# Attention steps inside a feed-forward loop: the weighted sum before the maximum, and finished outputs handled as an item begins

## The reference

```python
def _diff_attend(q1, q2, k1, k2, v, q_pos, k_pos, lam):
    ...
    def probs(q, k):
        s = jnp.einsum('bqhd,bkhd->bhqk', q.astype(jnp.float32), k.astype(jnp.float32)) * scale
        return jax.nn.softmax(jnp.where(mask, s, NEG_INF), axis=-1)

    w = probs(q1, k1) - lam * probs(q2, k2)
    return jnp.einsum('bhqk,bkhe->bqhe', w, v.astype(jnp.float32))
...
    f = (jax.nn.silu(h @ lw['ffn_w_gate']) * (h @ lw['ffn_w_up'])) @ lw['ffn_w_down']
```

## Time and profile before

| | us |
|---|---|
| median of 3 runs | 3170.92 |
| lowest, highest | 3169.41, 3175.09 |
| profiled execution, its own time | 3174.06 |
| its span | 3172.3 |
| PE busy | 2966.4 (94%) |
| DVE busy | 1779.2 (56%) |
| ACT busy | 1375.5 (43%) |
| POOL busy | 220.2 (7%) |

### The profile page before, as it was taken

One profiled execution on the slowest core, in us unless ns is written; L12 is line 12 of the kernel. 1 busy time (PEld: TensorE's weight loads), 2 busy tenths in 40 slices (PEclk: granted clock), 3 DMA queues, 4 the chain that ended last, 5 costly groups with the idle time before them and its releaser, 6 DMA issues.

```text
span 3172.3 us, 38465 instructions
## 1 busy us (share of the span) xinstructions
PE 2966.4 (94%) x14384; PEld 2413.3 (76%) x14384; DVE 1779.2 (56%) x2858; ACT 1375.5 (43%) x2500; POOL 220.2 (7%) x314
## 2 busy tenths in 40 slices
PE   6999999759999999999999999899999999999997
PEld 5788787547768777777877787778788777787875
DVE  5767745357626666566565556655666555333454
ACT  4655635344224444554444445544444444222233
POOL 0101100110000000001000100001111000000000
PEclk9999989868999999999999999999999999999998
DMA  5546332546754443454443334534332244232221
GB/s 159 182 140 222 133 134 73 150 135 228 217 150 116 123 113 113 154 159 120 116 114 105 108 101 155 162 103 130 100 114 76 96 167 126 80 97 84 86 74 59
DMA packets 377720, 402.65 MB, mean 127 GB/s; under 512 B 25657, under 2 KB 277989, under 8 KB 377536
## 3 DMA queue, kind: packets, MB, share of 16 engines
q1 hardware_dynamic: 360768, 341.38, 36.5%
q0 software_dynamic: 16768, 58.81, 4.8%
HBM read 341.26 MB, written 58.91 MB: 126 GB/s over the span
## 4 chain that ended last, share of the span: by engine, by line
PE 60%; DVE 11%; ACT 3%; issue 2%; DMA 0%; SPq 0%; DVEq 0%; ACTq 0%; POOL 0%; POOLq 0%
PE c_bank L2582 48%; PE b_S L2874 3%; PE b_WT L2886 2%; DVE c_w L2262 2%; PE b_O L2900 2%; DVE b_m L2462 1%; PE b_S L2591 1%; PE b_O L2591 1%; ACT c_junk L2034 1%; DVE c_rows L2273 1%; DVE c_rows L2280 1%; PE b_S L2854 1%; PE b_O L2902 1%; DVE c_act L2374 1%; DVE b_p L2469 1%
## 5 line engine op out<-in xcount | busy, mean ns | idle before, releaser
L2582 PE MATMUL c_bank<-c_hT,c_w 128*128 128x512 f32 (+1 forms) x4416 | 1036.8, 389 | 14.9 <-DVE c_hT L2300 14.9
L2582 PEld LDWEIGHTS c_bank<-c_hT,c_w 128*128 128x128 f32 x4416 | 802.0, 192 | 171.9 <-issue 17.7
L2262 DVE TENSOR_TENSOR c_w<-c_raw,c_w 128x1024 fp32r<-128x1024 f32 x334 | 405.5, 1220 | 198.2 <-ACT c_w L2013 196.9
L2582 PE MATMUL c_bank<-c_w,c_fT 128*128 128x512 f32 x2112 | 506.7, 393 | 0.0
L2013 ACT ACTIVATE c_w<-c_raw 128x1024 fp32r<-128x1024 f32 x334 | 351.1, 1055 | 290.2 <-PE c_bank L2582 246.3
L2582 PEld LDWEIGHTS c_bank<-c_w,c_fT 128*128 128x128 f32 x2112 | 391.7, 188 | 87.3 <-issue 3.4
L2191 ACT ACTIVATE b_p<-b_S,b_nm 128x512 f32<-128x512 f32 (+3 forms) x288 | 180.0, 630 | 518.6 <-DVE b_nm L2463 518.6
L808 PE MATMUL a_bank<-a_w,a_hT 128*128 128x512 f32 (+1 forms) x1224 | 300.1, 401 | 0.0
L2582 PE MATMUL c_bank<-c_w,c_hT 128*128 128x512 f32 x1152 | 270.4, 393 | 7.7 <-DVE c_w L2262 4.0
L808 PEld LDWEIGHTS a_bank<-a_w,a_hT 128*128 128x128 f32 (+1 forms) x1224 | 220.6, 183 | 61.3 <-issue 3.8
L2582 PEld LDWEIGHTS c_bank<-c_w,c_hT 128*128 128x128 f32 x1152 | 217.9, 190 | 54.8 <-DVE c_w L2262 4.4
(11 more groups left out here) (362 smaller groups left out, 3391.2 us busy)
## 6 DMA issues: line engine op xcount, KB each, us to landing
c_raw<-in_ffn_w_gate SPq DMA_DIRECT2D x88, 512.0 KB, 4.9
c_raw<-in_ffn_w_up SPq DMA_DIRECT2D x88, 512.0 KB, 4.1
c_raw<-in_ffn_w_down SPq DMA_DIRECT2D x88, 512.0 KB, 4.3
a_raw<-in_w_in SPq DMA_DIRECT2D x40, 1024.0 KB, 5.1
b_k<-split_kT SPq DMA_DIRECT2D x72, 256.0 KB, 4.9
b_v<-split_v SPq DMA_DIRECT2D x36, 512.0 KB, 3.6
c_raw<-in_w_out SPq DMA_DIRECT2D x32, 512.0 KB, 5.0
c_raw<-in_ple_w_gate SPq DMA_DIRECT2D x32, 512.0 KB, 4.4
```

What stands on the lines that cost most here:

```text
L2262: V.tensor_tensor(w[:, e[1] % SLOTS, 1], raw[:, n % RAW], w[:, e[1] % SLOTS, 0].bitcast(F32), ALU.subtract).then_inc(split_ready, 1)
L2582: ins = T.matmul(out, lhs(k, a), rhs(k, b), start=first and k == 0 and n == 0, stop=end and k == blocks - 1 and n == 2)
```

## The change

In both attention stages VectorE's weighted sum of the older step moves ahead of the maximum of the new one. In `feed`, the copy `ob` and the addition to `o` of a finished tile move from behind the transposed weights to the very top of the item, on ScalarE and on VectorE; the square and the root stay behind the transposed weights but go ahead of the copy `fT` of the feed-forward block. No instruction is added or taken away.

```diff
@@ attend_first, vector @@
             for t in range(END):
+                s = t - ADD
+                if 0 <= s < NSTEP:
+                    i, kc, n = tile_of[s], STEPS[s][3], size(s)
+                    dve.wait_ge(t2_ready, s + 1)
+                    V.scalar_tensor_tensor(p[:, s % PRING, 0, 0:n], p[:, s % PRING, 0, 0:n], coef[:, i % TRING, 0, kc:kc + 1],
+                                           p[:, s % PRING, 1, 0:n], ALU.mult, ALU.add).then_inc(w_ready, 1)
                 if t < NSTEP:
...
-                s = t - ADD
-                if 0 <= s < NSTEP:
...
@@ feed, scalar @@
+                x = finished(n, 1)
+                if x is not None:
+                    act.wait_ge(pv_done, last_step[x] + 1)
+                    wait_if_any(act, o_ready, x)
+                    A.activation(ob[:], O[:, 0, 1], ACT.Copy).then_inc(ob_ready, 1)
                 if was == ("mix0", 3):
...
                     A.activation(wT[:, 0, 0:size(s)], WT[:, 0:size(s)], ACT.Copy).then_inc(wt_hi, 1)
-                if was[0] in ("up", "far"):
-                    b = was[1]
-                    bank, count = job[j, "up", b]
-                    act.wait_ge(acc_free[bank], count)
-                    A.activation(fT[:, b % 8, 0], act1[:, b % 2], ACT.Copy).then_inc(f_hi, 1)
                 x = finished(n, 1)
                 if x is not None:
-                    act.wait_ge(pv_done, last_step[x] + 1)
-                    wait_if_any(act, o_ready, x)
-                    A.activation(ob[:], O[:, 0, 1], ACT.Copy).then_inc(ob_ready, 1)
                     act.wait_ge(o_ready, x + 1)
...
+                if was[0] in ("up", "far"):
+                    b = was[1]
+                    bank, count = job[j, "up", b]
+                    act.wait_ge(acc_free[bank], count)
+                    A.activation(fT[:, b % 8, 0], act1[:, b % 2], ACT.Copy).then_inc(f_hi, 1)
@@ feed, vector @@
+                x = finished(n, 1)
+                if x is not None:
+                    dve.wait_ge(ob_ready, x + 1)
+                    if x >= 4:
+                        dve.wait_ge(o_turned, x // 4)
+                    V.tensor_tensor(o[:, x % 4], O[:, 0, 0], ob[:], ALU.add).then_inc(o_ready, 1)
                 if was == ("mix0", 3) and last:
...
+                s = valued(n)
+                if s is not None:
+                    g, h, t, kc = STEPS[s]
+                    x, c = tile_no(g, h, t), size(s)
+                    dve.wait_ge(t2_ready, s + 1)
+                    V.scalar_tensor_tensor(p[:, s % PRING, 0, 0:c], p[:, s % PRING, 0, 0:c], coef[:, x % TRING, 0, kc:kc + 1],
+                                           p[:, s % PRING, 1, 0:c], ALU.mult, ALU.add).then_inc(wc_ready, 1)
                 s = scored(n)
                 if s is not None:
...
                     V.tensor_scalar(nm[:, x % TRING, :, kc], m[:, x % TRING, :, kc], -QSCALE, None, ALU.mult).then_inc(nm_ready, 1)
-                s = valued(n)
-                if s is not None:
...
                 x = finished(n, 1)
-                if x is not None:
-                    dve.wait_ge(ob_ready, x + 1)
-                    if x >= 4:
-                        dve.wait_ge(o_turned, x // 4)
-                    V.tensor_tensor(o[:, x % 4], O[:, 0, 0], ob[:], ALU.add).then_inc(o_ready, 1)
                 s = scored(n)
```

## The result

The changed kernel took 3207.81 us (median of 4 runs, 3205.02 to 3209.07) beside 3170.44 for the kernel before (4 runs, 3169.41 to 3175.09): ratio 1.0114, 95% interval 1.0096 to 1.0131. It is slower by 37 us; the forecast was 20 slower, 3191, with 3173 to 3209 as its range, so the time lies 1 us inside the upper end. The profiled execution's span went from 3172.3 to 3205.9 us, by 33.6.

The account below looks back on a forecast made before the run. Largest single cause of TensorE's waits: transposes waiting for VectorE's weighted sum, 41.0 us in 35 waits. Terms: 19 + 16 + 3 - 13 - 5 = +20 us, giving 3191 us against the median, range 3173 to 3209.

Parts of the forecast that it names:

- the step: ScalarE's queue: `ob` at the top delays tanh and weight copy; value products wait 30 to 50 us for the low half.
- Finishing items after "up": 20 items right after a query tile's last value products, with tanh: tanh starts late, 0.96 us each, 19 us lost.
- The other finishing items: 24 items without tanh: weight copy behind `ob`, value products 0.72 us late each; 16 us lost (8 to 19).
- Heads: Four items after "up" that finish a head's fourth tile: `fT` behind the root costs 0.8 us each, 3 us lost.
- Rival 3: Slower by more: new stops halve the clock after them in each of 20 items, 31 us more, 3222 us; chance 0.05.
- The five long waits and the clock: TensorE's transposes where head outputs were just turned: 2.5 us gained from shorter waits, 5 us from less slow clock.
- The swap elsewhere: Sum ahead of maximum, outside finishing items: 4.8 us gained in eight other waits, 3.4 in a dozen late steps.
- First stage: `attend_first`, 16 steps with the sum ahead of the maximum: no net effect, 0 us, 4.8 either way.
- Rival 1: Faster: sum ahead of maximum pays in full, early finish is covered; 35 us gained, 3136 us; chance 0.12.
- Rival 2: No change: the 24 finishing items without tanh cost nothing, their weight copy being otherwise covered; +4 us, 3175 us; chance 0.12.
- rival 4: Moving the sum gains nothing, since it waits for POOL where it waited for the maximum; 3209 us; chance 0.03.

Follow-up runs that it names:

- the two kernels with the finish in the middle: Changed kernel with `ob` behind tanh and split, addition behind maximum, `fT` ahead of square and root: 3144.34 us; the same with maximum ahead of sum: 3162.62 us.
- the swap alone: Kernel before with only the weighted sum moved ahead of the maximum, in both attention stages: 3175.58 us, ratio 1.0012.

## Why the prediction was right, and where its sizes were off

The direction, the mechanism and the signs named beforehand came true: the wait for the sum fell to 26.2 (forecast 20 to 28), a wait for the low half appeared, 28.5 us (just under the forecast's 30 to 50, well over the 15 that would have spoken against the step), tanh stands behind `ob` and the products behind the addition. One part of a sign did not: behind tanh the wait for the sum was to grow, and in the items after "up" it went from 9.7 us to 9.2; the loss there shows at the value products, 12.4 us where there was none, and at the heads' turnings. The forecast came out 17 us low: 11 of it lie in the terms below, some 2 outside the items; the rest is what the profiled executions stand off their medians. That the time still lies in the range, by 1 us, is partly luck: two terms went past their own upper bounds (the other finishing items 20.7 against 19, the heads 8.1 against 5), while the items after "up" came out near their lower one. The range's lower end was also added up wrongly: it takes 19 for the items after "up", whose own lower bound is 15, and by its own terms would be -1, or 3170.

- *Finishing items after "up", 19.* Right in its chain, a little high: from tanh to the value products 8.00 us (forecast 8.10), from scores 8.37 (8.59), mostly because tanh starts 0.17 after the copy does and not after its end. 0.74 each instead of 0.96.
- *The other finishing items, 16.* Measured 20.7. The chain was right, but the durations came from items in which POOL was not busy. The 18 plain ones lose 17.1 us; with POOL's product cut they lose 12.4, 0.69 each against the forecast's 0.72. The moved instructions now fall beside POOL's.
- *Heads, 3.* This is the term that failed most. I took 0.8 in each of four items for `fT` behind the root; undoing that place alone brought 8 us, 5.6 of them in these heads and their turnings. The stop at the turning grew (1.62 to 2.09 us in the head shown, beside the new 0.60 ahead of it), and the clock fell where it had not fallen before: 17 us at the lower level in the ten items of this row of the table, none before the change. Rival 3 had this mechanism in the wrong place: not in all 20 items but at the turnings, where the stops are longest. That the pair of stops lowers the clock is read from these rows, not tried by itself.
- *The five long waits and the clock, 2.5 + 5.* Measured 7.4. The waits fell from 3.7 to 2.35 us; time at the low level in these items fell from 17 to 10 us, not to nothing, and the waits gave the rest.
- *The swap elsewhere, 8.* Measured 5.5; the three short turnings' 2 were lost under the late heads. The swap's full size is shown where nothing stands in its way, 18 us between the two kernels with the finish in the middle.
- *First stage, 0.* Shown.

Rival 1 (faster) was to be decided on VectorE, to whose chain the finish was to add no more than 0.53 us. By the item shown and that of the earlier trace rows it adds 1.53: the first product with tanh starts 1.08 us after the scores (1033.11 and 1032.03), where it started 0.45 ahead of them. The run with both steps in the middle adds nothing ahead of the sum, and is faster, by 29 us where the rival had 35. Rival 2 fell with the other finishing items, rival 4 with the wait's fall; in the change the sum waits 0.0 us for POOL.

I was wrong about the swap alone, after the prediction, and the reading comes from the prediction itself: it calls the 1.20 us at the low half the only cover of the chain. In a finishing item the addition comes later still and releases the same value products; there the cover was 0.40 us. The change itself was spared this, since it moves the addition to the top.

## What to carry to other kernels

An instruction placed first in an engine's list holds all that stands behind it until its input comes; move a step up only to a place where its input is already there and the engine would otherwise wait. Where two engines feed one chain, undo both moves before you judge either: each alone showed 7 and 23 us, both together (with `fT`) 63. And list everything that releases the late instruction, since a wait taken off one input uncovers the next. Compare item by item: an average of 0.74 us, equal to the change's, hid a gain in twelve items and a loss in four.

## What was not expected of the hardware

VectorE and POOL slow each other. In the trace of the change the 128x512 sum took up to 1.18 us beside POOL's product and 0.75 alone, the 128x1024 split up to 1.70 and 1.22 alone; POOL's product took 0.70 us on average where it met neither (85 of 108) and 1.25 where it met one (23), at most 1.79. The maximum, which reads only PSUM, was not stretched (1214 ns in the six that met POOL's product, 1220 in the others), nor the first product with tanh, one of whose two inputs is in PSUM (687 and 688 ns). The page "SBUF — State Buffer" of the Trainium skill (Who interferes with whom) says that a VectorE instruction with two SBUF inputs contends with a GpSimd instruction that reads SBUF, and that one with at most one such input, outside its two-port modes, does not; the rows agree in which instructions are stretched. Its rule that the later one is blocked wholly was not tried here.

The clock fell behind a pair of stops (0.60 and 2.09 us) in a head where one stop of 1.62 us had left it at full speed. With 0.60 and 1.49 it still fell, for 3.4 us instead of 6.8. Whether the pair or the sum decides was not tried.
